# State-space decode updates by feature: transposes of a held column and a per-feature scalar in place of masked outer products

## The chip, the cores and the metric

The kernel runs on one core of a Trainium2 chip. TensorE (PE in the profile) multiplies and transposes, VectorE (DVE) and ScalarE (ACT) do elementwise work, GpSimd (POOL) does elementwise work and issues stores, SyncE (SP) issues the weight loads. The metric is the time of one execution in microseconds. All data is float32.

## The reference, cut to what matters

One inference step of a two-layer decoder, on 256 prompt tokens and, at the same time, on 8 sequences that each add one token (the decode tokens). Layer 0 holds a gated linear attention with 4 heads (GLA) and a state-space part with 16 heads in 2 groups (SSD); layer 1 holds another gated recurrence; both end in a mixture of 16 experts. The change touches only the SSD state of the 8 decode tokens. For one token, sequence b and head h, with a state of 128 rows (the features of B) by 64 columns (the features of x):

```
dt  = softplus(dt + dt_bias)                 # one number per head and sequence
S   = S * exp(dt * A) + outer(B, x * dt)     # B: 128, shared by the 8 heads of a group; x: 64 per head
y   = C @ S                                  # C: 128, shared by a group
```

So each of the 8 sequences and 2 groups has a state tile of 128 rows by 512 columns (8 heads of 64) to which an outer product is added: 16 tiles in all.

## The kernel before, in words

Everything is written out by hand: each engine has its own instruction list, and semaphores tie the lists together. Activations lie with features on partitions and tokens along the row: A[:, chunk, token], 264 tokens of which the last 8 (NP to T) are the decode tokens. The eight PSUM banks are used by number.

PE's list in layer 0 is this. First come small projections and the first chunks of the big input projection. Then come the 4 GLA heads, the 2 SSD groups and the output projection. Between the pieces of heads and groups PE is fed with the rest of the input projection: feed(n) (L717, the matmul is L725) issues n of its float32 matmuls of 264 columns, each of which the profile records as two. So PE nearly always has work while other engines prepare the next piece.

Three places matter here.

**The decays by token** (decays_token_major, L879 to L898), after the first GLA head has been turned. It brings the step sizes dt and their sums from head-major rows (dtT, 16 heads on partitions) to token-major columns in bank 6: L885 to L887 are transposes, L889 and L893 are matmuls that spread one column over 128 partitions. L887 makes dt of the 8 decode tokens, 8 rows by 16 heads. ACT copies the bank out (L1500 to L1503), POOL waits for these copies, and 12 feed matmuls follow.

**The head of an SSD group** (L906 to L924). PE transposes B (L913), the decode columns of B (L914, to 8 rows), the x of the prompt (L918), the decode columns of x (L920, 8 rows by 512), and forms the scores (L923). ACT copies the transposed B (L1518 for the decode rows, L1519). DVE then multiplies x by its steps (L1921, L1922), the decode rows by theirs (L1924), masks the scores (L1926) and lays out eight masked copies of B (L1928): 8 rows by 8 times 128, where copy b is zero but for row b. POOL has cleared the other rows of both (L629, L630) ahead of the store of the GLA states. PE meanwhile spreads the decay sums of one pair of heads (spread_g, L930), runs 8 feed matmuls and waits for DVE (ssd_tm_copied, L954).

**The decode updates** (decode_updates, L942): for each of the 8 sequences one matmul of the masked copy b with the 512 columns of x times dt (L947), into bank 7 or 5 in turn, which gives the outer product on 128 partitions; three feed matmuls follow. DVE adds the bank to the state tile (L1956), between pieces of the convolution in group 0. From the third sequence on PE waits for the addition two sequences back. After the eighth, PE goes on to the state of the prompt (L967, L972), one chunk of feed and the outputs (L983), for which DVE must have made the decayed scores (L1975).

The GLA heads in the same kernel already add their decode updates in the form that the change brings here: transposes of a broadcast column (L792) and one DVE instruction with a per-partition scalar (L1833).

The lines that are replaced, and the place where PE waits in a group:

```
pe.matmul(bank[7 - 2 * (b % 2)][:, :], s_bmask[:, b, :], s_xdec[:, :], start=True, stop=True
          ).then_inc(sem("ssd_dec_ready"), 1)
feed(3)
```

Of the kernel before, what the change touches and what calls it, by code (L numbers as in the profile page):

```python
# [7 lines left out]
ALU = mybir.AluOpType  # L8
# [3 lines left out]
P = 128  # L12
D = 1024
DC = D // P
NP = 256
NB = 8
T = NP + NB
# [63 lines left out]
def trunk_program(nc, ins, outs):  # L81
# [4 lines left out]
    with ExitStack() as ctx:  # L86
# [5 lines left out]
        def sem(name):  # L92
            if name not in sems:
                sems[name] = ctx.enter_context(nc.semaphore(name))
            return sems[name]
# [6 lines left out]
        A = sb("A", [P, AB_CHUNKS, T])  # L102
# [25 lines left out]
        def area(base, *shape):  # L128
            n = 1
            for s in shape:  # L130
                n *= s
            assert base + n <= W.shape[1]
            v = W[:, base:base + n]
            if len(shape) == 2:
                v = v.rearrange("p (a b) -> p a b", a=shape[0])
            if len(shape) == 3:
                v = v.rearrange("p (a b c) -> p a b c", a=shape[0], b=shape[1])
            return v
# [357 lines left out]
        s_S = area(4608, NCS, 512)  # L496
        s_eg = area(5632, 512)
        s_yi = area(6144, 512)
        s_xdec = area(6656, 512)
        s_bdec = area(7168, P)  # L500
        s_bmask = area(7296, NB, P)
        s_read = area(8320, 2, 512)
        s_sq = area(9344, 4, T)
        s_tm = area(10400, 4, 16)
        s_w = area(10464, 2, 16)
        s_el = area(10496, 2, 16)
        s_dd = area(10528, 16)
        s_egd = area(10544, NB, 16)
        dtT_rows = sb("dtT", [P, 3, T])
        dtT = dtT_rows[0:16]  # L510
# [3 lines left out]
        def _(pool):  # L514
# [111 lines left out]
            gate_head_gla(0)  # L626
            prompt_states_stored(4)
            stage_end(pool, 1)
            st.add(pool.memset(s_xdec[:, :], 0.0))  # L629
            st.add(pool.memset(s_bmask[:, :, :], 0.0))  # L630
            st.settle()
            pool.sem_inc(sem("ssd_rows_cleared"), 1)
            store_states(GLA_ST0, 4, gla_s, "gla_stored")
            gate_head_gla(1)
            for g in range(2):
# [55 lines left out]
        def _(pe):  # L691
# [187 lines left out]
            def decays_token_major():  # L879

                pe.wait_ge(sem("dt_steps"), 2)
                t = bank[6]
                for c in range(NCS):
                    s = slice(c * CS, (c + 1) * CS)
                    pe.transpose(t[:, 16 * c:16 * c + 16], dtT[:, 1, s], ident[0:16, 0:16])  # L885
                    pe.transpose(t[:, 32 + 16 * c:48 + 16 * c], dtT[:, 0, s], ident[0:16, 0:16])
                pe.transpose(t[0:NB, 64:80], dtT[:, 0, NP:T], ident[0:16, 0:16])  # L887
                for c in range(NCS):
                    pe.matmul(t[:, 80 + 16 * c:96 + 16 * c],  # L889
                              dtT[:, 1, (c + 1) * CS - 1:(c + 1) * CS].to_broadcast([16, P]), ident[0:16, 0:16],  # L890
                              start=True, stop=True)
                for b in range(NB):
                    mm = pe.matmul(t[:, 112 + 16 * b:128 + 16 * b],  # L893
                                   dtT[:, 2, NP + b:NP + b + 1].to_broadcast([16, P]), ident[0:16, 0:16],
                                   start=True, stop=True)
                mm.then_inc(sem("tm_steps"), 1)
                feed(12)
                pe.wait_ge(sem("tm_steps"), 2)  # L898
# [7 lines left out]
            for g in range(2):  # L906
# [4 lines left out]
                for c in range(NCS):  # L911
                    s = slice(c * CS, (c + 1) * CS)
                    pe.transpose(bank[4][:, 256 + c * P:256 + (c + 1) * P], BT[:, s], ident[:, :])  # L913
                pe.transpose(bank[7][0:NB, 0:P], BT[:, NP:T], ident[:, :])  # L914
                for c in range(NCS):
                    s = slice(c * CS, (c + 1) * CS)
                    for j in range(4):
                        pe.transpose(bank[1 + c][:, j * P:(j + 1) * P], A[:, XS0 + 4 * g + j, s], ident[:, :])  # L918
                for j in range(4):
                    pe.transpose(bank[3][0:NB, j * P:(j + 1) * P], A[:, XS0 + 4 * g + j, NP:T], ident[:, :])  # L920
                for c in range(NCS):
                    s = slice(c * CS, (c + 1) * CS)
                    mm = pe.matmul(bank[4][:, c * P:(c + 1) * P], BT[:, s], CT[:, s], start=True, stop=True)  # L923
# [18 lines left out]
                def decode_updates(b0):  # L942

                    for b in range(b0, b0 + 4):
                        if b >= 2:
                            pe.wait_ge(sem("ssd_dec_updated"), NB * g + b - 1)
                        pe.matmul(bank[7 - 2 * (b % 2)][:, :], s_bmask[:, b, :], s_xdec[:, :], start=True, stop=True  # L947
                                  ).then_inc(sem("ssd_dec_ready"), 1)
                        feed(3)

                spread_g(0)
# [372 lines left out]
        def _(act):  # L1324
# [172 lines left out]
            def copy_decays():  # L1497
                act.wait_ge(sem("tm_steps"), 1)
                t = bank[6]
                st.add(act.copy(s_tm[:, :, :], t[:, 0:64].rearrange("p (a h) -> p a h", h=16)))  # L1500
                st.add(act.copy(s_dd[0:NB, :], t[0:NB, 64:80]))
                st.add(act.copy(s_el[:, :, :], t[:, 80:112].rearrange("p (a h) -> p a h", h=16)))
                st.add(act.copy(s_egd[:, :, :], t[:, 112:240].rearrange("p (a h) -> p a h", h=16)))  # L1503
                st.settle()
                act.sem_inc(sem("tm_steps"), 1)
                take_ab(6)
                take_ab(7)
# [7 lines left out]
            act.sem_inc(sem("w_steps"), 1)  # L1515
            for g in range(2):
                act.wait_ge(sem("ssd_turned"), g + 1)
                st.add(act.copy(s_bdec[0:NB, :], bank[7][0:NB, 0:P]))  # L1518
                st.add(act.copy(s_btm[:, :, :], bank[4][:, 256:512].rearrange("p (c k) -> p c k", k=P)))  # L1519
                st.settle()  # L1520
                act.sem_inc(sem("ssd_btm_copied"), 1)
                m0 = AB_SSD + 6 * g
                take_ab(m0)
                for pr in range(4):
                    act.wait_ge(sem("ssd_diffs"), 4 * g + pr + 1)
                    for c in range(NCS):
                        e = s_E[:, c, 2 * pr:2 * pr + 2, :]
                        st.add(act.activation(e, e, ACT.Exp))
                    if pr in (0, 2):
                        take_ab(m0 + 1 + pr // 2)  # L1530
                st.settle()
                act.sem_inc(sem("ssd_exps"), 1)
                if g == 0:
                    conv_tanh([10, 11])
                take_ab(m0 + 3)
                take_ab(m0 + 4)
                act.wait_ge(sem("ssd_update_ready"), 2 * g + 1)
                st.run(act.copy(s_S[:, 0, :], bank[7][:, :]))
                act.sem_inc(sem("ssd_state0"), 1)
                act.wait_ge(sem("eg_steps"), 2 * g + 1)  # L1540
                st.run(act.copy(s_eg[:, :], bank[5][:, :]))
                act.sem_inc(sem("eg_steps"), 1)
                for i in range(2):
                    act.wait_ge(sem("ssd_reads_ready"), 2 * g + i + 1)
                    act.copy(s_read[:, i, :], bank[5 + 2 * i][:, :]).then_inc(sem("ssd_reads_copied"), 1)
                    if i == 0:
                        take_ab(m0 + 5)
                act.wait_ge(sem("ssd_gated"), g + 1)
                st.run(act.activation(s_sq[:, :, :], A[:, XS0 + 4 * g:XS0 + 4 * g + 4, :], ACT.Square,
                                      scale=NORM_SSD ** -0.5))  # L1550
                act.sem_inc(sem("ssd_squared"), 1)
# [136 lines left out]
        def _(dve):  # L1688
# [223 lines left out]
            for g in range(2):  # L1912
# [6 lines left out]
                for c in range(NCS):  # L1919
                    xp = h8(bank[1 + c][:, :])  # L1920
                    st.add(dve.tensor_tensor(h8(s_xdt[:, c, :]), xp, per_head(s_tm[:, 2 + c, hs], P), ALU.mult))  # L1921
                    st.add(dve.tensor_tensor(h8(s_xw[:, c, :]), xp, per_head(s_w[:, c, hs], P), ALU.mult))  # L1922
                dve.wait_ge(sem("ssd_rows_cleared"), 1)
                st.add(dve.tensor_tensor(h8(s_xdec[0:NB, :]), h8(bank[3][0:NB, :]), per_head(s_dd[0:NB, hs], NB), ALU.mult))  # L1924
                dve.wait_ge(sem("ssd_btm_copied"), g + 1)
                st.add(dve.tensor_tensor(s_g0[:, :, :], bank[4][:, 0:256].rearrange("p (c t) -> p c t", t=P),  # L1926
                                         causal[:, :].rearrange("p (o t) -> p o t", o=1).to_broadcast([P, NCS, P]), ALU.mult))
                st.add(dve.tensor_tensor(  # L1928
                    s_bmask[0:NB, :, :], s_bdec[0:NB, :].rearrange("p (o k) -> p o k", o=1).to_broadcast([NB, NB, P]),
                    ident[0:NB, 0:NB].rearrange("p (b o) -> p b o", o=1).to_broadcast([NB, NB, P]), ALU.mult))  # L1930
                st.settle()
                dve.sem_inc(sem("ssd_tm_copied"), 1)
                def sums_read(of):
# [18 lines left out]
                def decode_states(b0):  # L1952
                    for b in range(b0, b0 + 4):
                        dve.wait_ge(sem("ssd_dec_ready"), NB * g + b + 1)
                        s = ssd_state(g, b)
                        dve.tensor_tensor(s, s, h8(bank[7 - 2 * (b % 2)][:, :]), ALU.add).then_inc(sem("ssd_dec_updated"), 1)  # L1956
                        if b != 3:
                            next(steps, None)
                        if g == 0 and b in (5, 6):
                            conv_silu(b + 3)  # L1960
# [369 lines left out]
```

## Time and profile before

| | us |
|---|---|
| three runs | 1084.03, 1091.43, 1091.7 |
| median of them | 1091.43 |
| the profiled execution | 1084.51 |
| its span on the core | 1082.7 |
| GLA heads, up to | 184 |
| SSD groups | 184 to 278 |
| experts of layer 0, from the first gather to the last matmul | 360 to 592 |
| experts of layer 1, likewise | 833 to 1066 |

The span is the stretch from the first to the last instruction; the time of the execution is 1.8 us more. Busy shares of the span: PE 96%, DVE 35%, ACT 26%, POOL 8%. The chain of waits, followed back from the last instruction, is PE for 88% of the span, DMA for 4%, DVE for 4%, ACT for 2%. A row of the chain gives the start, the time that the chain spends there, and what is done; a row of the timeline gives start, length, engine, line, and, in brackets, how long the engine had been idle before and what ended that.

### The profile page before, as it was taken

How to read it: one execution, taken by the hardware profiler on the slowest of the kernel's cores; microseconds unless marked ns; L12 is line 12 of the kernel's file. 1: busy time of each engine (PE TensorE's matmuls, PEld its weight loads, DVE VectorE, ACT ScalarE, POOL GpSimd, SP SyncE). 2: the span in 40 equal slices, each digit the busy share in tenths (PEclk: the TensorE clock that was granted, in tenths of full speed). 3: DMA queues.
4: the chain of work that ended last, by engine and by line, in shares of the span. 5: the costliest groups of instructions: out<-in, count | busy, mean ns of one | idle time of the engine just before them, and what ended most of it. 6: DMA issues, size and time to landing. Idle time of an engine off the chain costs nothing.

```text
span 1082.7 us, 13250 instructions
## 1 busy us (share of the span) xinstructions
PE 1036.3 (96%) x5295; PEld 668.7 (62%) x5295; DVE 374.0 (35%) x926; ACT 283.5 (26%) x588; POOL 82.6 (8%) x136
## 2 busy tenths in 40 slices
PE   8999989999998999999999799999998999999996
PEld 5878767677786635454545687777786454545433
DVE  1256764663302402121213335555315221111114
ACT  2444333222202211000001337766405100000002
POOL 1111111213100000000000000011300000000000
PEclk9999999999999999999999899999998999999999
DMA  9632224432675299999999542222394799999991
GB/s 374 264 130 83 83 83 182 197 166 90 253 301 194 102 423 413 422 421 421 421 421 428 218 156 84 81 84 83 106 370 188 308 421 415 420 421 420 421 395 41
DMA packets 35649, 284.28 MB, mean 263 GB/s; under 512 B 4184, under 2 KB 5592, under 8 KB 6264
## 3 DMA queue, kind: packets, MB, share of 16 engines
q1 hardware_dynamic: 33552, 268.52, 61.2%
q0 software_dynamic: 1536, 14.32, 3.2%
q8 instruction: 46, 0.75, 0.3%
q10 hardware_dynamic: 496, 0.53, 0.2%
q14 instruction: 19, 0.16, 0.1%
HBM read 268.05 MB, written 15.40 MB: 262 GB/s over the span
## 4 chain that ended last, share of the span: by engine, by line
PE 88%; DMA 4%; DVE 4%; ACT 2%; issue 1%; POOL 0%; DVEq 0%; ACTq 0%
PE bank L1132 18%; PE bank L725 14%; PE bank L1156 9%; PE bank L1293 6%; PE bank L1026 5%; PE bank L1168 5%; PE bank L1117 5%; DMA ring<-in_w_up 4%; PE bank L1280 4%; PE bank L1046 2%; PE bank L1060 2%; PE bank L781 2%; PE bank L1054 1%; PE bank L947 1%; PE bank L792 1%; PE bank L811 1%
## 5 line engine op out<-in xcount | busy, mean ns | idle before, releaser
L1132 PE MATMUL bank<-ring,A 128*64 128x512 f32 x880 | 223.0, 592 | 2.4 <-issue 1.7
L725 PE MATMUL bank<-xT,ring 128*128 128x264 f32 x704 | 171.1, 392 | 0.0
L725 PEld LDWEIGHTS bank<-xT,ring 128*128 128x128 f32 x704 | 131.5, 192 | 34.0 <-issue 14.6
L1132 PEld LDWEIGHTS bank<-ring,A 128*64 128x64 f32 x880 | 73.8, 137 | 124.1 <-issue 124.1
L1156 PE MATMUL bank<-ring,W 128*64 128x512 f32 x448 | 113.4, 595 | 0.9 <-ACT W L1614 0.9
L2174 DVE TENSOR_TENSOR W<-W,bank 128x512 f32<-128x512 f32 x16 | 11.0, 687 | 204.4 <-PE bank L1132 204.4
L1293 PE MATMUL bank<-xT,ring 128*128 128x264 f32 x320 | 81.4, 391 | 0.0
L1156 PEld LDWEIGHTS bank<-ring,W 128*64 128x64 f32 x448 | 34.9, 137 | 60.9 <-issue 59.8
L1168 PE MATMUL bank<-W,A 128*128 128x264 f32 x256 | 63.5, 393 | 1.7 <-issue 1.7
L1132 PE MATMUL bank<-A 128*64 128x512 f32 x144 | 63.5, 592 | 0.7 <-DMA ring<-in_w_up 0.7
L1293 PEld LDWEIGHTS bank<-xT,ring 128*128 128x128 f32 x320 | 56.7, 190 | 9.4 <-issue 1.6
L1168 PEld LDWEIGHTS bank<-W,A 128*128 128x128 f32 x256 | 46.2, 190 | 21.1 <-issue 14.7
L1026 PE MATMUL bank<-A,ring 128*128 128x264 f32 x256 | 58.2, 386 | 0.0
L2189 DVE TENSOR_TENSOR W<-W,bank 128x264 f32<-128x264 f32 x128 | 54.6, 428 | 9.3 <-PE bank L1168 8.0
L1026 PEld LDWEIGHTS bank<-A,ring 128*128 128x128 f32 x256 | 48.6, 190 | 8.2
L661 POOL TENSOR_SCALAR xT<-xT,vecs 128x264 f32<-128x264 f32 x4 | 5.6, 1395 | 607.2 <-DVE xT L2028 607.2
L1117 PE MATMUL bank<-A,W 128*128 128x224 f32 x256 | 51.1, 359 | 0.3 <-DVEq L2123 0.3
L2181 DVE COPY A<-bank 128x512 f32<-128x512 f32 x16 | 11.1, 691 | 114.1 <-PE bank L1156 114.1
L1117 PEld LDWEIGHTS bank<-A,W 128*128 128x128 f32 x256 | 49.2, 194 | 1.2 <-DVEq L2123 0.5
L1598 ACT ACTIVATE W<-bank 128x512 f32<-128x512 f32 x16 | 9.6, 597 | 153.9 <-PE bank L1132 153.9
L1280 PE MATMUL bank<-xT,ring 128*128 128x264 f32 x192 | 44.8, 396 | 2.5 <-ACT xT L1570 2.2
L1280 PEld LDWEIGHTS bank<-xT,ring 128*128 128x128 f32 x192 | 37.0, 194 | 10.0 <-issue 2.6
(309 smaller groups left out, 1215.1 us busy)
## 6 DMA issues: line engine op xcount, KB each, us to landing
ring<-in_w_gate SPq DMA_DIRECT2D x56, 1024.0 KB, 13.3
ring<-in_w_down SPq DMA_DIRECT2D x56, 1024.0 KB, 13.3
ring<-in_w_up SPq DMA_DIRECT2D x54, 1024.0 KB, 16.5
ring<-in_w_ab SPq DMA_DIRECT2D x11, 2048.0 KB, 7.6
ring<-in_w_c SPq DMA_DIRECT2D x8, 2048.0 KB, 13.8
A<-in_w_up SPq DMA_DIRECT2D x10, 1024.0 KB, 13.3
ring<-in_w_oab SPq DMA_DIRECT2D x4, 2048.0 KB, 10.3
A<-in_w_gate SPq DMA_DIRECT2D x8, 1024.0 KB, 12.6
```

The costliest lines, as they stand in the source:

```text
L725: mm = pe.matmul(ab_bank(m)[:, 0:T], slot(AB_IN0 + m // 4, 8)[:, c, (m % 4) * P:(m % 4 + 1) * P], xT[:, c, :], start=(c == 0), stop=(c == ...
L781: mm = pe.matmul(bank[c // per][:, (c % per) * dv:(c % per + 1) * dv], hb["ktm"][0:C, c, :], hb["vtm"][0:C, c, 0:dv], start=True, stop=True)
L1026: mm = pe.matmul(out_bank(m)[:, 0:T], w[:, c, (m % 2) * P:(m % 2 + 1) * P], src, start=(c == 0), stop=(c == 15))
L1046: mm = pe.matmul(out_bank(m)[:, 0:T], w[:, c, (m % 4) * P:(m % 4 + 1) * P], A[:, 16 + c, :], start=(c == 0), stop=(c == 7))
L1060: mm = pe.matmul(bank[7][:, 0:T], ones[:, :], lnsq[:, c, :], start=(c == 0), stop=(c == DC - 1))
L1117: mm = pe.matmul(gather_bank(i)[:, c * 4 * PCAP:(c + 1) * 4 * PCAP], xtm[:, b, (2 * i + c) * P:(2 * i + c + 1) * P], SLOT1[:, b, 4 * g:4 * ...
L1132: mm = pe.matmul(bank[i][64 * j:64 * j + 64, :], xg[:, 2 * (pair % 2) + j, c, :], slot(n0 + 6 * pair + 2 * i + j, 8)[:, c, :], start=(c == ...
L1156: mm = pe.matmul(bank[4 + i][64 * j:64 * j + 64, :], hT[:, f * P + CAP * j:f * P + CAP * (j + 1)], slot(n0 + 6 * pair + 4 + j, 8)[:, 4 * i ...
L1168: pe.matmul(back_bank(c)[:, 0:T], Y[:, c * P:(c + 1) * P], PT[:, pair, :], start=True, stop=True).then_inc(sem("moe_back"), 1)
L1280: mm = pe.matmul(c_bank(m)[:, 0:T], slot(n, 8)[:, c, i * P:(i + 1) * P], xT[:, c, :], start=(c == 0), stop=(c == DC - 1))
L1293: mm = pe.matmul(c_bank(m)[:, 0:T], slot(c_in(m // 4), 8)[:, c, (m % 4) * P:(m % 4 + 1) * P], xT[:, c, :], start=(c == 0), stop=(c == DC - 1))
L2189: dve.tensor_tensor(xacc[:, c, :], xacc[:, c, :], back_bank(c)[:, 0:T], ALU.add).then_inc(sem("moe_added"), 1)
```

## The change

Three edits that belong together.

1. In the decays by token, the transpose of dt to 8 rows is replaced by 16 matmuls that spread dt of each head over the 64 partitions of its features: a column of the identity, broadcast to 64 columns, times the head rows of dt, 8 columns each. ACT copies them out (128 by 64 numbers in place of 8 by 16).
2. In the head of a group, the decode columns of B and x are no longer transposed. One DVE instruction multiplies the 4 by 8 decode columns of x, as they lie, by their steps. The copy of the 8 rows of B, the masked copies and the two clearing instructions of POOL with their semaphore go.
3. In the decode updates, the matmul of 512 columns becomes four transposes of one column of x times dt, broadcast to 128 columns, which put it on every partition, 128 features each. DVE multiplies by B as a per-partition scalar and adds the state in one instruction.

```diff
@@ areas
-        s_xdec = area(6656, 512)
-        s_bdec = area(7168, P)
-        s_bmask = area(7296, NB, P)
+        s_xdec = area(6656, 4, NB)
+        s_dtf = area(10808, 8, NB)
...
@@ POOL, after the GLA heads
             stage_end(pool, 1)
-            st.add(pool.memset(s_xdec[:, :], 0.0))
-            st.add(pool.memset(s_bmask[:, :, :], 0.0))
-            st.settle()
-            pool.sem_inc(sem("ssd_rows_cleared"), 1)
             store_states(GLA_ST0, 4, gla_s, "gla_stored")
@@ PE, decays by token
-                pe.transpose(t[0:NB, 64:80], dtT[:, 0, NP:T], ident[0:16, 0:16])
+                for j in range(8):
+                    for i in range(2):
+                        pe.matmul(t[64 * i:64 * i + 64, 240 + NB * j:240 + NB * (j + 1)],
+                                  ident[:, 2 * j + i:2 * j + i + 1].to_broadcast([P, 64]), dtT_rows[:, 0, NP:T],
+                                  start=True, stop=True)
@@ PE, head of a group
-                pe.transpose(bank[7][0:NB, 0:P], BT[:, NP:T], ident[:, :])
...
-                for j in range(4):
-                    pe.transpose(bank[3][0:NB, j * P:(j + 1) * P], A[:, XS0 + 4 * g + j, NP:T], ident[:, :])
@@ PE, decode updates
-                        pe.matmul(bank[7 - 2 * (b % 2)][:, :], s_bmask[:, b, :], s_xdec[:, :], start=True, stop=True
-                                  ).then_inc(sem("ssd_dec_ready"), 1)
+                        for j in range(4):
+                            tr = pe.transpose(bank[7 - 2 * (b % 2)][:, j * P:(j + 1) * P],
+                                              s_xdec[:, j, b:b + 1].to_broadcast([P, P]), ident[:, :])
+                        tr.then_inc(sem("ssd_dec_ready"), 1)
                         feed(3)
@@ ACT
-                st.add(act.copy(s_dd[0:NB, :], t[0:NB, 64:80]))
+                st.add(act.copy(s_dtf, t[:, 240:240 + 8 * NB].rearrange("p (j b) -> p j b", b=NB)))
...
-                st.add(act.copy(s_bdec[0:NB, :], bank[7][0:NB, 0:P]))
@@ DVE, head of a group
-                dve.wait_ge(sem("ssd_rows_cleared"), 1)
-                st.add(dve.tensor_tensor(h8(s_xdec[0:NB, :]), h8(bank[3][0:NB, :]), per_head(s_dd[0:NB, hs], NB), ALU.mult))
+                st.add(dve.tensor_tensor(s_xdec, A[:, XS0 + 4 * g:XS0 + 4 * g + 4, NP:T], s_dtf[:, 4 * g:4 * g + 4, :], ALU.mult))
...
-                st.add(dve.tensor_tensor(
-                    s_bmask[0:NB, :, :], s_bdec[0:NB, :].rearrange("p (o k) -> p o k", o=1).to_broadcast([NB, NB, P]),
-                    ident[0:NB, 0:NB].rearrange("p (b o) -> p b o", o=1).to_broadcast([NB, NB, P]), ALU.mult))
@@ DVE, decode updates
-                        dve.tensor_tensor(s, s, h8(bank[7 - 2 * (b % 2)][:, :]), ALU.add).then_inc(sem("ssd_dec_updated"), 1)
+                        dve.scalar_tensor_tensor(s, h8(bank[7 - 2 * (b % 2)][:, :]), A[:, B0 + g, NP + b:NP + b + 1], s,
+                                                 ALU.mult, ALU.add).then_inc(sem("ssd_dec_updated"), 1)
```

## Rows read from the trace of the kernel before

**Rows 1.** The page: the chain that ended last, by engine.
```profile
PE 88%; DMA 4%; DVE 4%; ACT 2%; issue 1%; POOL 0%; DVEq 0%; ACTq 0%
```

**Rows 2.** The chain of waits, group 0: start us, us, what.
```profile
184.72 0.11 PE bank L914
...
185.70 0.44 PE bank L920 x4
...
189.18 0.59 DVE W L1924
...
190.10 1.74 DVE W L1928
...
197.56 0.86 PE bank L947 x2
198.41 1.34 PE bank L725 x6
```

**Rows 3.** Timeline at group 0's wait, with the idle time before.
```profile
192.03 1.10 PE L930 MATMUL bank<-dtT,ident 128*128 128x256 f32 x4 [1.02 <-DVEq L1932]
```

**Rows 4.** The chain of waits, head of group 1.
```profile
230.79 0.11 PE bank L914
...
232.26 0.85 PE bank L920 x4
...
238.74 1.10 PE bank L930 x4
...
241.62 0.86 PE bank L930 x4
```

**Rows 5.** The chain of waits: four transposes, small matmuls of several shapes.
```profile
41.62 1.79 PE bank L893 x16
...
164.65 0.44 PE bank L792 x4
...
216.82 1.02 PE bank L972 x16
...
219.83 1.90 PE bank L983 x32
```

**Rows 6.** DVE's updates in the two loops, by tile: duration ns min/median/max.
```profile
L1833 DVE SCALAR_TENSOR_TENSOR ring<-bank,A,ring x30: 473/480/485, 63.3 to 171.1; 128x256 f32<-128x256 f32 x30
```

**Rows 7.** Timeline of group 0's loop and what follows it.
```profile
198.45 0.69 DVE L1956 TENSOR_TENSOR ring<-ring,bank 128x512 f32<-128x512 f32 x1 [1.51 <-PE bank L947]
...
200.72 0.69 DVE L1956 TENSOR_TENSOR ring<-ring,bank 128x512 f32<-128x512 f32 x1
...
202.84 0.69 DVE L1956 TENSOR_TENSOR ring<-ring,bank 128x512 f32<-128x512 f32 x1 [0.24 <-PE bank L947]
...
205.11 0.69 DVE L1956 TENSOR_TENSOR ring<-ring,bank 128x512 f32<-128x512 f32 x1 [0.52 <-PE bank L947]
...
214.67 0.69 DVE L1956 TENSOR_TENSOR ring<-ring,bank 128x512 f32<-128x512 f32 x1 [1.16 <-PE bank L947]
...
216.43 2.59 DVE L1975 TENSOR_TENSOR W<-W 128x1024 f32<-128x1024 f32 x2
```

**Rows 8.** Busy by window; the last three numbers: granted clock, DMA share, GB/s.
```profile
42.00:43.00 1.00, 1.00 (x11) 1.00 (x10) 0.00 (x0) 0.00 (x0) 0.00 (x0) 1.00 1.04 442
44.00:45.00 1.00, 1.00 (x4) 0.79 (x3) 0.00 (x0) 0.00 (x0) 0.92 (x1) 0.50 0.92 393
231.50:235.00 3.50, 3.50 (x16) 2.97 (x15) 2.58 (x3) 1.60 (x3) 0.47 (x1) 0.56 0.00 0
184.00:187.00 3.00, 2.72 (x22) 2.56 (x23) 0.69 (x3) 0.91 (x5) 2.11 (x4) 1.00 1.01 431
355.00:371.00 16.00, 13.79 (x81) 10.85 (x81) 10.59 (x29) 4.34 (x6) 0.00 (x0) 1.00 0.00 1
```

**Rows 9.** The chain of waits, last pair of experts of each layer.
```profile
549.98 22.02 DMA ring<-in_w_up
...
1024.05 22.02 DMA ring<-in_w_up
```

More of the change, by code:

```diff
@@ L506, in trunk_program @@
         s_el = area(10496, 2, 16)
-        s_dd = area(10528, 16)
         s_egd = area(10544, NB, 16)
```

## The prediction

> **What bounds the kernel now.** I read the chain of waits by engine first, since it says whose instructions can be worth anything: 88% of the span hangs on PE, 4% on DMA [rows 1]. Then I read the same chain in order of time over the SSD groups (184 to 278 us). There almost every piece is a PE piece that follows another without a gap, with one exception: in group 0 the chain leaves PE, runs over DVE's list L1921 to L1928, and comes back to PE at 192.03 us [rows 2, 3]. So in this stage an instruction taken from PE's list shortens the path by its own length, and one taken from DVE's list does so only up to PE's idle time there, 1.02 us [rows 3]. For the experts I read the windows and the chain: before them the DMA engines are idle (share 0.00 from 355 to 371 us, [rows 8]), because every buffer is full, and each layer ends in a wait of the same 22.02 us for weights [rows 9]. The weight stream restarts when PE has read its first buffers and then takes its fixed time; PE reaching that point earlier moves the stream, the wait and the end by the same amount. So what the SSD stage gains should arrive whole.
>
> **Part 1, the decode updates.** The matmul with a masked copy costs the chain 0.86 us, in two records [rows 2]; there are 16. In its place come four transposes with 128 columns each. The GLA heads hold the very form: four transposes of a broadcast column between feed matmuls take 0.44 us [rows 5]. That is 0.42 us saved per update, and 16 x 0.42 = 6.7 us, all on PE's path if DVE keeps up.
>
> Does DVE keep up? Its addition becomes multiply and add with a scalar per partition. At 256 columns this form takes 0.48 us [rows 6]; no row has it at 512. The 512-column addition takes 0.69 us [rows 7]. Bounds for the new one are no change and twice the 256-column row, 0.96 us; I take 0.75, since the fixed part is paid once. In group 1 DVE does little else in the loop. In group 0 it also carries the convolution. PE's period falls from 0.86 + 1.34 = 2.20 us to 0.44 + 1.34 = 1.78 us [rows 2, 5]. DVE's first update starts at 198.45 and the second at 200.72 with no idle time, so it needs 2.27 us for the first, and 205.11 - 200.72 less 0.24 (idle before the third) and 0.52 us idle before the fourth, thus 3.6 us for the next two [rows 7]. It would begin the fourth 5.9 us after the first, PE offers it after 3 x 1.78 = 5.3 us. DVE is late by 0.6 us, yet PE waits only for the update two sequences back, and DVE has caught up by the time of the spread and the fifth. At the end of the loop DVE had 1.16 us of idle time before the eighth update, of which 0.42 goes. From there to the decayed scores its work is unchanged: L1975 ends at 219.02 [rows 7], and the chain reaches PE's L983 at 219.83 [rows 5]; that distance loses nothing but the few hundredths by which the new instruction is longer, since the eighth transposes end 0.42 us earlier after their own start and all else on PE is the same. Cost taken: none; bound: 16 x 0.27 = 4.3 us if each 0.96 us lay open on the path, which the idle times of 1.5 us in the loop exclude for all but a few, so 0.5 us for the range.
>
> **Part 2, the heads of the groups.** Group 0: L914 and L920 go, 0.11 + 0.44 = 0.55 us [rows 2]. On DVE L1928 goes (1.74 us), and L1924 (0.59 us) becomes an instruction over 32 columns of SBUF; I take 0.2 us, between nothing and the 0.59 of the row it replaces. DVE's signal then comes 0.55 + 1.74 + 0.39 = 2.68 us earlier, PE's own work 0.55 us earlier; the wait of 1.02 us is gone with over 0.6 us to spare. Gain: 0.55 + 1.02 = 1.57 us. Next late there is nothing: PE runs on its feed.
>
> Group 1: L914 is 0.11 us. L920 costs 0.85 us [rows 4], not 0.44, because it falls into 3.5 us with a granted clock of 0.56, most of it at the 1.2 GHz level [rows 8]. If that low stretch ends when it did, other work fills it, and the removal is worth the 0.44 us of group 0; the upper bound is 0.85. I take 0.44. PE's L930 at 238.74 takes 1.10 us against 0.86 for the next one [rows 4]: 0.24 us of waiting for DVE, which goes. Gain: 0.79 us.
>
> Removed at no gain: ACT's copy of B's rows lies beside PE's first spread; POOL's two clearings lie ahead of a store whose buffers the output projection needs much later, so that store merely starts about 1.5 us sooner, when the DMA engines are busy at 1.01 with it anyway [rows 8]. The clearing had hidden nothing else.
>
> **Part 3, the steps by feature.** Added to PE at about 41 us: 16 matmuls with a 64-column stationary operand and 8 moving columns, thus 32 records as all float32 matmuls here have two; one transpose of 0.03 us goes, and is left out of the sum. No row has 8 columns with 64. Lower bound: nothing, if they hid wholly beside loads of the next; upper bound: L893, whose 16 records with a 128-column stationary operand and 16 moving columns take 1.79 us, 0.112 each, hence 3.6 us. The nearest rows have the same 64 columns, alternate halves of the array as here, but 128 moving columns: 1.02 / 16 = 0.064 and 1.90 / 32 = 0.059 us [rows 5]. As the load sets the pace I take 0.06, so 32 x 0.06 = 1.9 us. PE is the chain here too, and it does not wait again for DVE or DMA before the first scores, so this lies on the path. ACT's copy grows from 16 to 64 columns beside 12 feed matmuls; PE asks for it only behind them: nothing.
>
> **Sum.** -6.7 - 1.57 - 0.79 + 1.9 = -7.2 us. Against the profiled execution's own 1084.5 us that is 1077.3. The three runs shown are 1084.03, 1091.43 and 1091.7, so the profiled one lies 6.9 us below their median; the sum applied to the median gives 1084.2 us.
>
> **Rivals.**
>
> *The clock falls in the loops* (slower). Four transposes of every ten records stand in the loop now. Against this, the head of group 0 holds 15 transposes in a row and its window shows a granted clock of 1.00 [rows 8]; for it, the clock did fall to 0.56 soon after the transposes of group 1 began, behind small matmuls and a wait. If the 16 periods, 16 x 1.78 = 28.5 us, ran at the 1.2 GHz level, they would take as long again: -7.2 + 28.5 = +21 us, 1113 us by the median. It decides once more than a quarter of the loops' time is spent low, where the loss passes 7.2 us. The Trainium skill, page "TensorE: Matmul & The Clock Gate", section Part 4 on the PE-mode transpose, speaks against the change: it says that transposes do not count as activity for the clock in the way matmuls do. By that rule the loops would lose all or part of what the transposes save; the window of group 0's head does not bear it out, that of group 1's neither shows nor excludes it. Chance 0.05.
>
> *The thin matmuls lengthen the low clock at the start.* Behind L885 to L893 the granted clock is 0.50 at 44 us after 1.00 at 42 us [rows 8], for some 3.3 us in all, which costs about half of that, 1.7. Two more microseconds of matmuls with 8 columns stand in just this place; should the low stretch double, the sum is -7.2 + 1.7 = -5.5 us, and with the thin matmuls themselves at the lower level up to 1 us more: -4.5, thus 1087 by the median. For it: the fall follows such matmuls. Against: only part of the stretch would be thin. Chance 0.20.
>
> *The weight stream hides it.* If the stream's start hung on its own earlier transfers, the saving would reappear as a longer wait at each layer's end, and the time would stay at 1091. The idle DMA window before each restart speaks against it. Chance 0.05.
>
> *More is gained*: group 1's low stretch of 3.5 us does not occur, as PE's work ahead of it changes its timing, worth another 1.7 us: -9, thus 1082.5. Chance 0.08.
>
> The forecast has the rest, 0.62.
>
> **The numbers.** Predicted: 1084 us. The forecast's own bounds run from -9.1 (thin matmuls free) to -5.0 (at L893's price and 0.5 us of DVE). What widens this more is that runs of one and the same kernel differ by 7 us here, the size of the effect: should the new median sit where the profiled execution did, it is 1077. The range 1076 to 1090 takes both, the second and the fourth rival; outside lie the clock rival, the stream rival and stray runs. A change of 1% is 10.9 us, about what a measurement of this kernel can tell from no change. -7.2 is within it; it shows as faster by more than 1% when the new median falls at the lower of the two places where runs lie. Faster 0.38, same 0.56, slower 0.06.
>
> **What the profile would show.** Four transposes of about 0.44 us in each of 16 places, at a granted clock of 1.00; PE without idle time ahead of L930 in group 0; the new DVE instruction near 0.75 us; the thin matmuls near 1.9 us in all; SSD groups from stage end to output projection 9 us shorter; both waits of 22 us unchanged. I would be wrong if the clock in the loops is 0.5, if L983 waits for DVE, if the thin matmuls take over 3 us, or if the 22 us have grown.

## The result, and the profile after

Four executions of each kernel, side by side: before 1084.03, 1091.43, 1091.7, 1082.03 us (median 1087.73); changed 1075.04, 1072.04, 1069.34, 1075.35 us (median 1073.54). The ratio is 0.9881, 95% interval 0.9844 to 0.9918: faster by 0.8 to 1.6%. I had forecast 1084 us with a range of 1076 to 1090 and a change within 1%. The direction was right, the time lies below the range. Over more executions, 88 later ones of the kernel before have a mean of 1084.8 us, and 21 of the changed kernel, these four among them, one of 1074.2 us: 10.6 us, or 1.0%. So some 3.6 us of the 14.2 us between the two medians above are the luck of four executions each. (Two executions that took far longer than all others, one of the kernel before at 2168.64 us and one of turn_back at 1402.42 us, are in no mean of this text.)

The profiled execution of the changed kernel took 1075.04 us, its span 1073.2. Chain by engine and the last waits:

```profile
PE 88%; DMA 4%; DVE 3%; ACT 2%; issue 1%; POOL 0%; DVEq 0%; ACTq 0%; POOLq 0%
```
```profile
544.39 21.50 DMA ring<-in_w_up
...
1015.09 21.56 DMA ring<-in_w_up
```

The same resources bound it as in [rows 1] and [rows 9]; the gain was not turned into a longer wait for weights.

The chain of waits of the changed kernel over group 0 and the heads of both groups (start us, us, what; L911, L915, L918, L925, L943, L719 are L913, L918, L923, L930, L947, L725 of before):

```profile
189.93 0.87 PE bank L915 x8
190.80 0.45 PE bank L918 x4
191.25 0.86 PE bank L925 x4
192.11 3.56 PE bank L719 x16
195.67 0.86 PE bank L925 x4
...
200.96 0.44 PE bank L943 x4
201.40 1.34 PE bank L719 x6
...
230.97 0.87 PE bank L915 x8
231.84 0.45 PE bank L918 x4
...
236.71 0.91 PE bank L925 x4
```

Against [rows 2 to 4]: the chain no longer leaves PE in group 0, each update costs 0.44 us for 0.86, and the head of group 1 runs at full speed (L918 is 0.45 us). Its twin before, L923, took nearly twice that:

```profile
233.12 0.85 PE bank L923 x4
```

DVE in the timeline of the changed kernel:

```profile
193.76 0.48 DVE L1919 TENSOR_TENSOR W<-A,W 128x32 f32<-128x32 f32 x1
194.17 0.41 DVE L1921 TENSOR_TENSOR W<-bank,causal 128x256 f32<-128x256 f32 x1
...
201.44 0.75 DVE L1948 SCALAR_TENSOR_TENSOR ring<-bank,A,ring 128x512 f32<-128x512 f32 x1 [1.09 <-PE bank L943]
...
213.55 0.75 DVE L1948 SCALAR_TENSOR_TENSOR ring<-bank,A,ring 128x512 f32<-128x512 f32 x1
...
216.89 2.59 DVE L1968 TENSOR_TENSOR W<-W 128x1024 f32<-128x1024 f32 x2
```

The update (L1948) takes the 0.75 us forecast. After its first update DVE is now nearly without idle time in group 0's loop, yet L1968, the decayed scores, ends at 219.48, and L980, PE's outputs that need them (L983 before), starts at 219.93 without a wait in the chain.

Now the chain by stretches, in these two profiles. These are the first instructions of group 0, of group 1 and of the output projection, before:

```profile
184.28 0.44 PE bank L913 x2
...
230.38 0.41 PE bank L913 x2
...
278.01 7.00 PE bank L1026 x31
```

and after:

```profile
189.49 0.44 PE bank L911 x2
...
230.55 0.41 PE bank L911 x2
...
272.43 7.23 PE bank L1023 x32
```

| stretch | before us | after us | change |
|---|---|---|---|
| start to first instruction of group 0 | 184.28 | 189.49 | +5.2 |
| group 0, to the same of group 1 | 46.10 | 41.06 | -5.04 |
| group 1, to the output projection | 47.63 | 41.88 | -5.75 |
| from there to the end of the span | 804.7 | 800.8 | -3.9 |

Group 0 is what the parts gave (1.57 + 8 x 0.42 = 4.93). The other rows are not, and here a second quantity comes in: stretches in which the granted clock is 0.50, the 1.2 GHz level. Of the +5.2 us ahead of group 0, the small matmuls that part 3 added are 1.0 (below), and the profile after has two such stretches there that the profile before lacks, about 1.7 us each.

Each execution's record has its span and mean granted clock. I split a span into **work**, span x clock, an estimate of the time it would take at full clock, and **loss**, span x (1 - clock). Both are somewhat rough. The clock is recorded to 0.001, which is 1.1 us of a single execution. And low clock where PE has nothing to do costs nothing; every profile ends so:

```profile
1077.60:1082.70 5.10, 0.00 (x0) 0.00 (x0) 1.89 (x6) 0.80 (x2) 0.00 (x0) 0.50 0.55 186
```
```profile
1068.70:1073.20 4.50, 0.00 (x0) 0.00 (x0) 1.37 (x4) 0.52 (x1) 0.00 (x0) 0.50 0.62 210
```

(before, then changed; PE is busy for 0.00 us, the clock is 0.50). So some 2.1 to 2.7 us of the loss in each of the nine profiles of the two kernels cost nothing; they are alike in both kernels and drop out of the differences.

| kernel | executions | span | work | loss |
|---|---|---|---|---|
| before | 88 | 1083.0 | 1068.3 +- 0.2 | 14.7 +- 0.35 |
| changed | 21 | 1072.4 | 1060.9 +- 0.2 | 11.5 +- 0.65 |

(means, with the error of the mean.) The work falls by 7.4 +- 0.3 us, the loss by 3.2 +- 0.7. The spread of runs within one kernel is mostly loss: the changed kernel's first four executions have spans of 1067.6 to 1073.6 at clocks of 0.993 to 0.988, and work of 1060.4 us with a standard deviation of 0.3. In the kernel before, work itself scatters more, by 1.6 us, beside 3.3 for the loss and 2.9 for the span.

### The profile page after: what moved, and what is told of

Read it like the earlier page. It is cut to its first block, busy times and chain, and to the rows that moved or that the text cites. A ratio compares the mean times of both kernels' runs of the same rounds, so it can differ in the third digit from the quotient of the medians.

```text
span 1073.2 us, 13349 instructions
## 1 busy us (share of the span) xinstructions
PE 1029.1 (96%) x5348; PEld 668.4 (62%) x5348; DVE 372.5 (35%) x924; ACT 283.2 (26%) x586; POOL 80.5 (8%) x134
## 4 chain that ended last, share of the span: by engine, by line
PE 88%; DMA 4%; DVE 3%; ACT 2%; issue 1%; POOL 0%; DVEq 0%; ACTq 0%; POOLq 0%
PE bank L1129 19%; PE bank L719 15%; PE bank L1153 9%; PE bank L1290 6%; PE bank L1023 5%; PE bank L1165 5%; PE bank L1114 5%; DMA ring<-in_w_up 4%; PE bank L1277 4%; PE bank L1043 2%; PE bank L775 2%; PE bank L1057 1%; PE bank L1051 1%; PE bank L786 1%; PE bank L805 1%; PE bank L800 1%
## 5 line engine op out<-in xcount | busy, mean ns | idle before, releaser
L719 PE MATMUL bank<-xT,ring 128*128 128x264 f32 x704 | 173.9, 396 | 0.0
L719 PEld LDWEIGHTS bank<-xT,ring 128*128 128x128 f32 x704 | 132.1, 195 | 27.2 <-issue 7.0
L1165 PEld LDWEIGHTS bank<-W,A 128*128 128x128 f32 x256 | 46.2, 190 | 21.1 <-issue 14.7
## 6 DMA issues: line engine op xcount, KB each, us to landing
ring<-in_w_gate SPq DMA_DIRECT2D x56, 1024.0 KB, 13.2
ring<-in_w_c SPq DMA_DIRECT2D x8, 2048.0 KB, 13.4
A<-in_w_gate SPq DMA_DIRECT2D x8, 1024.0 KB, 12.6
```

The costliest lines, as they stand in the source:

```text
L719: mm = pe.matmul(ab_bank(m)[:, 0:T], slot(AB_IN0 + m // 4, 8)[:, c, (m % 4) * P:(m % 4 + 1) * P], xT[:, c, :], start=(c == 0), stop=(c == ...
L1165: pe.matmul(back_bank(c)[:, 0:T], Y[:, c * P:(c + 1) * P], PT[:, pair, :], start=True, stop=True).then_inc(sem("moe_back"), 1)
```

## The experiments

Each of those in this table is an edit of the changed kernel. Span, work and loss are means over all its executions; the difference is to the changed kernel's 1072.4, 1060.9 and 11.5.

| run | executions | span | work | loss | difference in work | in loss |
|---|---|---|---|---|---|---|
| loop_matmul | 12 | 1079.6 | 1066.7 +- 0.5 | 13.0 +- 0.8 | +5.8 | +1.5 |
| loop_thrice | 12 | 1089.2 | 1074.6 +- 0.5 | 14.6 +- 1.2 | +13.7 | +3.1 |
| no_thin | 6 | 1070.9 | 1059.3 +- 0.5 | 11.6 +- 0.8 | -1.6 | +0.1 |
| thin_thrice | 12 | 1076.5 | 1062.9 +- 0.4 | 13.6 +- 0.8 | +2.0 | +2.1 |
| thin_spread | 10 | 1075.8 | 1063.2 +- 0.2 | 12.6 +- 1.0 | +2.3 | +1.1 |
| head_back | 9 | 1077.0 | 1063.8 +- 0.3 | 13.3 +- 1.1 | +2.9 | +1.8 |
| turn_back | 9 | 1075.6 | 1062.0 +- 0.3 | 13.6 +- 0.4 | +1.1 | +2.1 |
| mask_back | 11 | 1075.6 | 1060.5 +- 0.5 | 15.1 +- 1.4 | -0.4 | +3.6 |
| shifted | 9 | 1075.8 | 1062.4 +- 0.3 | 13.4 +- 0.9 | +1.5 | +1.9 |

**again, again2, again3: the changed kernel as it is.**

> The changed kernel once more, five rounds beside the kernel before, to size the change. Theory A (the change is worth about 8 us of PE work and waiting at full clock, and what was seen beyond that is time spent at the 1.2 GHz level, which falls by chance): ratio near 0.992, 8 to 9 us, with an interval that holds it; runs of one kernel differ by up to 7 us and, in each run, the span less half of (1 - granted clock) x 2 x span is the same within 1 us. Theory B (the change also removes low-clock stretches each time, as the one at the head of group 1): ratio near 0.988 again, about 13 us, and a higher mean granted clock for the changed kernel than for the one before.

Measured: 1074.85 us, ratio 0.9896 (0.9862 to 0.993); work 1061.1 us, with a standard deviation of 0.8 us in eight executions whose spans run from 1067.4 to 1076.1. Neither theory had it whole: the work is A's, and the clock is higher, as B had it.

> The changed kernel a third time, to size the change and the place of its low stretches. Theory A of the first runs has turned into this: 7 us of work at full clock (span x granted clock, 1068.0 against 1060.9) and 2 to 4 us of clock. So 9 to 11 us, ratio 0.990 to 0.992; the low stretch at 43 to 51 us doubled again; none at the head of group 1.

Measured: ratio 0.99 (0.9867 to 0.9933). Both low stretches stand at 43 to 51 us, none at group 1's head. The profile of again3, one more execution (1077.18 us), has its low stretches in the same places.

**loop_matmul: part 1 undone on PE.**

```diff
-                        for j in range(4):
-                            tr = pe.transpose(bank[7 - 2 * (b % 2)][:, j * P:(j + 1) * P],
-                                              s_xdec[:, j, b:b + 1].to_broadcast([P, P]), ident[:, :])
+                        tr = pe.matmul(bank[7 - 2 * (b % 2)][:, :].rearrange("p (c t) -> p c t", c=2), ident[:, :],
+                                       xT[:, 0:2, 0:NP], start=True, stop=True)
```

> The changed kernel with one float32 matmul of 512 columns (the identity as stationary operand, x as moving one, so that the decode states of the SSD part are left wrong) in place of the four transposes of each decode update: part 1 undone on PE alone. At 0.42 us each the 16 updates take back 6.7 us against the changed kernel, so by theory A the two SSD groups are 6.7 us longer (83.0 to 89.7 us) and the ratio to the kernel before is near 0.998 with the changed kernel at 0.992. By theory B it is the same, since the low stretches belong to the heads. If the transposes held back the clock, the cost would be under 3 us.

It leaves the decode states wrong and keeps the time of the matmul. The chain has 0.86 us for each update again; the work rises by 5.8 +- 0.5 us against 6.7 expected, the span by 7.2. This is the largest part of the change.

**loop_thrice: do transposes hold the clock down?**

```diff
-                        for j in range(4):
+                        for j in range(12):
```

(with j % 4 for the column and the place).

> The changed kernel with each group of four transposes issued three times in a row (same result). If transposes do not lower the clock: each update takes 1.31 us in place of 0.44, the loops are 16 x 0.87 = 14 us longer, and the granted clock in them is 1.00. If transposes do not count as activity, then with half of the loop's time in transposes the granted clock falls to 0.5 in the loops: the extra is 14 us plus up to 16 x 2.65 = 42 us.

Twelve transposes take 1.31 us of each 2.65 us of the loop. The chain of waits, and the windows over group 0's loop and most of group 1's (of the last three numbers the first is the granted clock):

```profile
204.86 1.31 PE bank L943 x12
...
207.50 1.31 PE bank L943 x12
```
```profile
200.00:218.00 18.00, 18.00 (x123) 16.34 (x122) 10.65 (x28) 4.38 (x13) 3.48 (x6) 1.00 0.22 72
240.00:260.00 20.00, 20.00 (x115) 17.67 (x113) 8.18 (x21) 4.20 (x13) 6.16 (x10) 0.98 0.33 122
```

The extra work is 13.7 us against 14, and the clock stays at the 2.4 GHz level with half of the time in transposes. (The 0.98 of the second window is the end of the low stretch at group 1's head, which stands at 237 to 241 us in this kernel, ahead of the loop.) So the clock rival is refuted for these loops. The Trainium skill, page "TensorE: Matmul & The Clock Gate", Part 4, says that transposes do not count as busy in the way matmuls do; for this mix of transposes and dense matmuls the trace does not agree, with a granted clock of 1.00. Whether transposes alone would hold the clock, no run here shows.

**no_thin, thin_thrice: the thin matmuls.** The first deletes the loop of 16 matmuls, the second repeats it three times.

> The changed kernel without the 16 thin matmuls that spread dt by feature (ACT copies other columns of the bank in their place, so dt is wrong for the decode states). By the trace of the changed kernel the 32 records take 1.03 us, so at equal clock it is 1.0 us faster than the changed kernel. If they lengthen or bring on the low clock behind them, as the second rival had it, it is 2 to 4 us faster on average and the feed matmuls behind take 7.2 us and not 8.45 us.

> The changed kernel with its 16 thin matmuls issued three times (same result). At 0.032 us a record the 64 extra records take 2.1 us. If a run of small matmuls is what brings on the low clock behind it, the low stretch here is as long or longer (two or three of about 3.4 us, 3.4 to 5.1 us lost) and span x (1 - clock) rises by 1 to 2 us; if it does not depend on their number, only the 2.1 us show.

The chains of waits of the changed kernel, of no_thin and of thin_thrice:

```profile
41.93 1.03 PE bank L883 x32
...
43.51 2.20 PE bank L891 x16
45.70 8.45 PE bank L719 x24
```
```profile
43.19 7.14 PE bank L719 x24
```
```profile
40.98 2.90 PE bank L883 x96
...
44.43 1.79 PE bank L891 x16
46.21 7.22 PE bank L719 x24
```

A thin record costs 0.032 us in the changed kernel (1.03 / 32) and 0.030 in thin_thrice (2.90 / 96), half of the 0.06 I had taken; work falls by 1.6 +- 0.5 without them and rises by 2.0 when they stand three times (expected 1.0 and 2.1). In the changed kernel the 12 feed matmuls behind them, 24 records, take 8.45 us for 7.2, and the windows show why, against [rows 8]:

```profile
43.00:44.00 1.00, 1.00 (x10) 1.00 (x10) 0.00 (x0) 0.00 (x0) 0.00 (x0) 1.00 0.96 410
45.00:46.00 1.00, 1.00 (x5) 0.96 (x5) 0.00 (x0) 0.26 (x3) 0.00 (x0) 0.50 0.95 410
...
49.00:50.00 1.00, 1.00 (x4) 0.79 (x3) 0.00 (x0) 0.38 (x1) 1.00 (x2) 0.50 0.00 0
```

Two low stretches in a row stand here in all four profiles of the changed kernel, one in four of five of the kernel before and in no_thin. So in these profiled executions the second rival is right at this place, about 1.7 us. But it is no simple matter of how many small matmuls: thin_thrice shows one stretch here. Nor is it fixed by the instructions: up to group 0 loop_matmul, loop_thrice, head_back, turn_back, mask_back and shifted have the same ones as the changed kernel, and here the profile of loop_matmul has no stretch, that of turn_back one, the others two. And over its 6 executions no_thin has the same loss as the changed kernel (11.6 against 11.5), so the second rival does not show in the means: the 2 to 4 us that it asked for came out as 1.5 us of span.

**thin_spread: nine feed matmuls moved between the small ones.**

> The changed kernel with nine of the twelve feed matmuls that follow the decays by token put between the small matmuls, two or four small groups apart (same result, same instructions). Both profiles of the changed kernel show 7 to 8 us at the 1.2 GHz level behind the small matmuls, 3.4 us lost. If the run of small matmuls in a row brings that on, it is gone or halved here: 1.7 to 3.4 us less than the changed kernel, 1070 to 1072 us. If any wait or small matmul nearby does it, no change.

```profile
42.83 0.33 PE bank L883 x8
43.16 0.64 PE bank L719 x2
43.80 0.33 PE bank L883 x8
```

Its profile has no low stretch there, but a feed matmul put singly between small ones takes 0.64 us in place of 0.445. Nine of them cost 1.8 us, the work rises by 2.3, the mean loss does not fall. Its mean span is 3.4 us longer than the changed kernel's, and of the kernels run here that compute the full result none has a shorter mean span than the changed one.

**head_back, turn_back, mask_back: part 2.** turn_back restores PE's transposes alone, mask_back only DVE's masked copies:

```diff
+                pe.transpose(bank[7][0:NB, 0:P], BT[:, NP:T], ident[:, :])
...
+                for j in range(4):
+                    pe.transpose(bank[3][0:NB, j * P:(j + 1) * P], A[:, XS0 + 4 * g + j, NP:T], ident[:, :])
```
```diff
+                st.add(dve.tensor_tensor(
+                    W[0:NB, 7296:7296 + NB * P].rearrange("p (b k) -> p b k", b=NB),
+                    causal[0:NB, :].rearrange("p (o k) -> p o k", o=1).to_broadcast([NB, NB, P]),
+                    ident[0:NB, 0:NB].rearrange("p (b o) -> p b o", o=1).to_broadcast([NB, NB, P]), ALU.mult))
```

head_back has both, ACT's copy and DVE's product over 8 rows.

> The changed kernel with the work of part 2 put back beside it (same result): per group the transposes of the decode columns of B and x on PE, ACT's copy of 8 rows, DVE's product over 8 by 512 and the eight masked copies, 8 by 1024. By the sum it costs 1.57 us in group 0 and 0.79 in group 1, 2.4 us at full clock (span x granted clock: 1060.9 us over 12 runs of the changed kernel to 1063.3). If the heads are also what brings the low clock to the kernel before (mean granted clock 0.9855 in 25 runs, 0.9897 in 12 of the changed kernel), its clock falls to about 0.986 and the time rises by some 6 us; if not, the clock stays near 0.990.

> The changed kernel with only PE's transposes of the decode columns put back in the heads (L914 and L920 of the kernel before; nobody reads them, same result). Work: 0.55 us per group, 1.1 us (span x granted clock near 1062.0). The low stretch at the head of group 1 stood in 3 of 3 profiles of the kernel before and in that with the whole heads put back, and in 0 of 5 with the new heads and loops no longer than before. If these transposes bring it, it is here again, and span x (1 - clock) is 1 to 2 us above the changed kernel's. If it falls by chance of timing, it may be absent.

> The changed kernel with only DVE's eight masked copies put back (8 by 1024 in a spare area, same result). DVE's signal in group 0 came 0.9 us before PE asked for it, so 1.74 us more make PE wait some 0.8 us there and 0.2 in group 1: 1 us in all (span x clock 1061.9). If the low stretch of group 1's head came from DVE's side, it is here again; by the record of where it starts, ahead of DVE's first instruction of the group, it is not.

The work is as summed for head_back (2.9 against 2.4) and turn_back (1.1 against 1.1). mask_back shows a wait of 0.49 us in group 0 in its timeline, but no more work over its 11 executions (-0.4 +- 0.5), a miss:

```profile
195.66 1.10 PE L925 MATMUL bank<-dtT,ident 128*128 128x256 f32 x4 [0.49 <-DVEq L1927]
```

The low stretch of group 1's head, in all five profiles of the kernel before, is in those of head_back, mask_back, thin_thrice and loop_thrice. It is in none of those of turn_back, loop_matmul, no_thin and thin_spread, nor in the four of the changed kernel. Windows of head_back and turn_back:

```profile
232.00:236.00 4.00, 3.68 (x19) 3.35 (x20) 2.85 (x3) 0.87 (x1) 1.90 (x2) 0.57 0.01 4
```
```profile
228.00:236.00 8.00, 8.00 (x47) 7.07 (x47) 7.10 (x14) 2.73 (x6) 1.46 (x2) 1.00 0.01 2
```

So the transposes that were removed do not bring it each time (one profile). Since kernels whose heads are the changed kernel's own have it too (thin_thrice, loop_thrice), nothing that part 2 took out is needed for it.

**shifted: the same instructions, 1.8 us later.**

```diff
+            for k in range(4):
+                pe.matmul(bank[3][:, 0:T], ident[:, :], xT[:, k, :], start=True, stop=True)
```

> The changed kernel with four dense float32 matmuls (8 records of 264 columns, 1.78 us) before group 0, which write a bank that nobody reads then (same result): everything behind moves by 1.8 us, nothing else changes. Work: 1060.9 + 1.8 = 1062.7 us. If where PE's low-clock stretches fall depends on when the sparse places come, and not on what the change removed, then span x (1 - clock), 11.4 us for the changed kernel, moves by 1.5 us or more, up or down, or a stretch appears at group 1's head. If it is the change's own doing, it stays at 11.4.

Work +1.5 (1.8 expected), loss +1.9 +- 1.1, and the stretch is back at group 1's head:

```profile
229.00:230.00 1.00, 1.00 (x12) 1.00 (x11) 0.00 (x0) 0.01 (x1) 0.92 (x3) 1.00 0.00 0
230.00:234.00 4.00, 3.13 (x17) 3.08 (x17) 3.36 (x6) 0.09 (x1) 2.62 (x4) 0.58 0.02 4
```

Ahead of it PE does what it does in the changed kernel. So a low stretch can come back at this place with the same instructions around it, when only dense work ahead of the groups was added (one profile).

**before_p1 to before_p4: where the kernel before is slow.**

> The kernel before once more, for where its time at the 1.2 GHz level lies. By theory A the stretches (each about 3.4 us, 1.7 us lost) lie at places both kernels share, in other places from run to run. By theory B one lies at the head of group 1 again, near 231 us.

> The kernel before once more, for the same: a low stretch at group 1's head near 231 us, and some 8 in all if the run is an average one.

Low stretches in single profiles, five of before (before, before_p1 to before_p4) and four of the changed kernel (about 1.7 us lost in each; the low clock behind PE's last work is not counted):

| place | before | changed |
|---|---|---|
| behind the small matmuls, 43 to 52 us | 1, 1, 0, 1, 1 | 2, 2, 2, 2 |
| third GLA head, about 155 to 165 | 0, 0, 1, 1, 1 | 1, 1, 1, 1 |
| group 1's head | 1, 1, 1, 1, 1 | 0, 0, 0, 0 |
| router of layer 0, about 341 to 367 | 0, 0, 0, 2, 2 | 1, 0, 0, 0 |
| between the layers, about 593 to 616 | 2, 2, 0, 1, 2 | 0, 2, 2, 2 |
| router of layer 1, about 812 to 840 | 2, 2, 2, 2, 2 | 2, 2, 2, 2 |

Theory B holds at group 1's head and theory A for the rest; the places are nearly always those where PE waits or does small matmuls, and both kernels have them. The four later profiles of the kernel before took 1083.58, 1079.25, 1086.69 and 1089.06 us; the last, expected to have some 8 stretches if average, has nine, with 18.5 us of loss by its record.

## Why the prediction was wrong

**The instructions were costed nearly right, in part by luck.** The sum was 7.2 us; the work fell by 7.4 +- 0.3. Part 1: 0.42 us each as forecast in the trace (6.7), 5.8 +- 0.5 when undone. Part 2: 1.57 us in group 0 was right with its mechanism, a wait of DVE that vanished; both heads together are 2.9 +- 0.3 of work against 2.4. One small price was off: L1919 takes 0.48 us, not 0.2, behind 0.9 us of cover. Part 3 was mis-sized: 1.03 us in the trace, not 1.9. I had taken as nearest the rows with the same 64-column load, 0.059 to 0.064 us a record, "as the load sets the pace"; those have 128 moving columns, and at 8 the record is half that, so the load did not set it. With 1.03 in place of 1.9 the sum is 8.1 us, further from the 7.4 than my 7.2 was. Part 3's error (0.9) and part 1's are of about the size of the errors of the work figures, so how the 7.4 divides is known no better than to some half microsecond each.

**What failed is the step from the sum to the time.** First, "If that low stretch ends when it did" (group 1) took TensorE's clock as given. The loss fell by 3.2 +- 0.7 us on top of the work. I had such a gain only as the fourth rival, 1.7 us at 0.08. Group 1's head fits that rival in the profiles (5.75 us gained for the 4.15 of the parts). The second rival came true in them too, and at these two places they cancel; so neither gives the 3.2 us of the means. Second, "the sum applied to the median": 1091.43 was the middle of three executions of which two lay near the kernel's slowest; over 88 the mean is 1084.8. From there 1084.8 - 7.2 = 1077.6 lies within the range I gave, and the 3.2 us of clock bring it to 1074.4, where the mean of 1074.2 was measured, outside the range. Third, the range took the low starting point and the fourth rival one at a time: together, 1084.5 - 7.2 - 1.7 = 1075.6, they already lie below its 1076. I named the 7 us between runs and did not ask what they were; in the later executions the granted clock stands beside each time and explains most of them.

**Right:** DVE keeps up, with 0.75 us an update; L980 does not wait; both waits for weights stayed, at 21.5 us for 22.0; the clock in the loops is 1.00; the gain in the SSD stage arrives at the end.

**Open:** why the changed kernel's mean loss is 3.2 us lower. shifted has a stretch at group 1's head that the changed kernel's profiles lack, and mask_back, turn_back and shifted, with no more than 1.5 us more work, each have about 2 to 3.6 us more loss. Each of these is known to about 1 us, but eight of the nine edits lie at +1.1 us or more. That fits with the changed kernel falling into favourable timing rather than with something it removed, but it is argued, not shown. The places of the loss do not settle it: nine single profiles average 10.9 us of placed loss before and 11.5 after, the other way round. One reason is which executions were profiled. By their own records the four of the changed kernel lost 13.7 us on average, against 11.5 over all 21, and none of its nine executions with a granted clock of 0.991 or more is among them; the five of before lost 13.2, against 14.7. So where the changed kernel's fast executions save their time was never seen. And no run puts back POOL's two clearings, which I had held to be worth nothing; what parts 1 and 2 gain when undone, less what part 3 costs (no_thin), is 5.8 + 2.9 - 1.6 = 7.1 of the 7.4 us of work, which leaves the clearings little.

## What to carry to other kernels

Where PE is the chain, compare work (span x granted clock) and loss apart: over some ten executions the first gives an edit's price to about half a microsecond where the times spread by 9 us, the second tells how much is clock. Before you explain a mean from a profile, check that the profiled execution is like the mean. In float32, replacing one matmul of 512 columns by four transposes of 128 halves the PE time, here 0.86 to 0.44 us, if the other factor can be applied as a scalar by the engine that reads the bank anyway. When the runs of a kernel differ by as much as the effect, find out what sets them apart before adding a sum to their median.

## What the runs showed that I had not expected

A float32 record with a 64-column stationary operand, its output to alternate halves of the partitions, and 8 moving columns costs 0.032 us; the 128-column ones with 16 moving columns cost 0.112. Low clock comes in stretches that each lose about 1.7 us, four to nine in a profile of the two kernels, at a few places; how many there are differs between executions of one kernel. A single feed matmul between groups of small ones costs 0.64 us instead of 0.445.
